# Linear attention's states: the order of the update and query matmuls, the engines of the first copies

## The chip, the cores and the metric

The kernel runs on one core of one Trainium2 chip. The metric is the device time of one execution in microseconds (us), as the median of some runs. Besides, one execution is profiled; its span is the time from its first to its last instruction.

## What is computed

A model of two blocks. The first block has a layer of gated linear attention with a dense feed-forward, then a layer of sliding-window attention with a mixture of eight experts; the second block is two layers of another attention. 256 tokens, width 1024. The change touches only the linear attention, in which the tokens are cut into four chunks of 64 and a state goes through the chunks, once forwards and once backwards (cut to what matters):

```python
def gla_chunked(q, k, v, log_a, inclusive):          # 4 heads, dk 128, dv 256, C = 64, n = 4 chunks
    ...
    chunk_update = jnp.einsum('bhnjk,bhnjv->bhnkv', k * jnp.exp(b_last - b), v)
    chunk_decay = jnp.exp(b_last[:, :, :, 0])
    def step(state, inp):
        decay, upd = inp
        return state * decay[..., None] + upd, state
    ...
    o_inter = jnp.einsum('bhnik,bhnkv->bhniv', q * jnp.exp(b), prev)
    return (o_intra + o_inter).reshape(B, H, S, dv)

o_f = gla_chunked(q, k, v, log_a_f, True)
o_b = flip(gla_chunked(flip(q), flip(k), flip(v), flip(log_a_b), False))
o = (o_f + o_b).transpose(0, 2, 1, 3)
o = o * lax.rsqrt(jnp.mean(o * o, axis=-1, keepdims=True) + NORM_EPS)
...
```

## The kernel before, in words

The program is written out by hand: each engine has its own list of instructions, in program order, and waits on semaphores that the others raise. A stage is a set of five functions (pe, act, dve, pool, sp). Nothing plans the order; the order in these functions is the order on the engine. Names: PE is the matrix engine, ACT the scalar engine, DVE the vector engine.

Weights come by DMA into slots, are split by ACT (L182) into a high part and by DVE (L192) into a low part, and every product with weights is three matmuls (`mm3`, L359, L360, L361). Most of the span is that.

In the linear attention (`make_gla`) the products within a chunk come first and leave their sums in four PSUM banks, `ob` = 1 to 4, two heads to a bank (L653). Then come the states. `S` holds the state of direction d (0 forwards, 1 backwards), 256 columns for each of four heads. There are three steps s. In step s direction 0 takes chunk c = s, direction 1 takes chunk c = 3 - s.

- PE `grow(s, d)` (L658): four matmuls, one a head, each over the 64 tokens of chunk c. They lie in partitions 0 to 63 where c is even and 64 to 127 where it is odd. The results go to PSUM banks 5 and 6 (d = 0) or 7 and 0 (d = 1), two heads to a bank. This is called an update block below (L668).
- DVE `grow(s, d)` (L822): in step 0 it copies the four results into `S` (L832), later it computes S x decay + result (L834). It raises `S_out(s, d)`.
- PE then multiplies the queries of the next chunk nx by `S` and adds the products to `ob` (L681). nx is s + 1 or 2 - s; the result has 64 columns of the array, and lies in PSUM partitions 0 to 63 or 64 to 127 by nx. This is called a query block below. It raises `crossed(s, d)`. All of it is in fp32 and each of these matmuls leaves two records in the trace.

PE's order is: update block (0,0), update block (0,1), and then for each s and d: query block (s,d), update block (s+1,d). Twelve blocks of four matmuls in all, and within each all four matmuls have the same chunk.

After the states, ACT squares the sums for the head norm, for tokens 128 to 255 first (j = 1, L439, waits for `crossed(2, 0)`) and then for tokens 0 to 127 (j = 0, waits for `crossed(2, 1)`). ACT and DVE make the inverse roots (L445, L449, L453), DVE scales (L846, `og`), PE transposes `og` (L418), ACT and DVE take the transposed parts into `xh` and `xl` (L424, L430), and PE goes on with the output projection (`gla out0`). ACT loads its table for the square root ahead of time (L763).

Two other places are spoken of. The scores of the sliding-window attention are written head after head, for each the three matmuls of `mm3` (L359, L360, L361) in turn; the first two of four heads lie in partitions 0 to 63, the other two in 64 to 127. And L708 is ACT's copy of a 128x256 result of PE out of PSUM.

Of the kernel before, what the change touches and what calls it, by code (L numbers as in the profile page):

```python
# [12 lines left out]
ACT = mybir.ActivationFunctionType  # L13
ALU = mybir.AluOpType
AX = mybir.AxisListType.X

D, T, FF, NE = 1024, 256, 2816, 8
# [108 lines left out]
def count_on(steps, names):  # L126

    return Steps(steps.sem, names, max(steps.n.values()))
# [71 lines left out]
def run(steps):  # L200
    for _ in steps:
        pass
# [8 lines left out]
def body(nc, ctx, I, out):  # L211
    count = [0]

    def sem(name):
        return ctx.enter_context(nc.semaphore(name))

    def steps(name, *names):
        return Steps(sem(name), names)
# [5 lines left out]
    psum = ctx.enter_context(nc.psum_tensor("psum", [128, 8, 512], F32))  # L224
# [320 lines left out]
    def make_gla(sc):  # L545
        qT = sb("qT", [128, 4, T], scope=sc)
        kT = sb("kT", [128, 4, T], scope=sc)
        v = sb("v", [128, 2, D], scope=sc)
# [7 lines left out]
        S = sb("S", [128, 2, D], scope=sc)  # L556
# [11 lines left out]

        ld_wg, s_wg0, s_sco0, s_one = sem("wg_landed"), sem("wg_zeroed"), sem("sco_zeroed"), sem("lr_one")
        DJ = [(d, j) for d in range(2) for j in range(2)]  # L570
        SD = [(s, d) for s in range(3) for d in range(2)]
        four = [(i,) for i in range(4)]
        q_out, k_out, lr_out = steps("gla_q", *four), steps("gla_k", *four), sem("gla_lr")
        z_acc, z_out = steps("gla_z_acc", *four), steps("gla_z", *four)
# [5 lines left out]
        prods = steps("gla_prods", *[(d, x) for d in range(2) for x in (0, 1, "k", "q", "kl", "qb")])  # L580
        intra = steps("gla_intra", *[(d, j, x) for d in range(2) for x in ("scores", "kl") for j in range(2)])
        sc_out, klN_out = steps("gla_sc", *DJ), steps("gla_klN", *DJ)
        o_acc, grown, S_out, crossed = sem("gla_o"), steps("gla_grown", *SD), steps("gla_S", *SD), steps("gla_crossed", *SD)

        OG = (4, 5, 6, 7, 0, 1, 2, 3)
        OB = (5, 6, 7, 3, 4, 2)
# [5 lines left out]

        def ch(ap):
            return ap.rearrange("p (g c) -> p g c", c=64)

        def sp(sp):
            for dst, src in ((wg[96:112, 0, :], I["gla_gate_w_fwd"][0]), (wg[112:128, 1, :], I["gla_gate_w_bwd"][0]),
# [13 lines left out]
        def pe(pe):  # L611
# [43 lines left out]
                                      start=h % 2 == 0, stop=False, skip_group_check=True)  # L655
            ins.then_inc(o_acc)

            def grow(s, d):  # L658
                c = s if d == 0 else 3 - s
                pp, j = (c % 2) * 64, c // 2  # L660
                bk = [5, 6] if d == 0 else [7, 0]
                pe.wait_ge(klN_out.at(d, 1), v_at)
                for h in range(4):
                    if s:
                        pe.wait_ge(S_out.at(s - 1, d))
                    else:
                        pe.wait_ge(klN_out.at(1, h // 2) if d == 0 else sc_out.at(1, h // 2))
                    ins = pe.e.matmul(psum[:, bk[h // 2], (h % 2) * 256:(h % 2) * 256 + 256],  # L668
                                      klN[pp:pp + 64, d, j, h * 128:(h + 1) * 128],
                                      v[pp:pp + 64, j, h * 256:(h + 1) * 256], start=True, stop=True)  # L670
                ins.then_inc(grown.end(s, d))

            grow(0, 0)
            grow(0, 1)
            for s in range(3):
                for d in range(2):
                    nx = s + 1 if d == 0 else 2 - s
                    op, oj = (nx % 2) * 64, nx // 2
                    pe.wait_ge(S_out.at(s, d), *qb_at[d])
                    for h in range(4):  # L680
                        ins = pe.e.matmul(psum[op:op + 64, ob[oj * 2 + h // 2], (h % 2) * 256:(h % 2) * 256 + 256],  # L681
                                          qb[:, d, h * T + nx * 64:h * T + nx * 64 + 64], S[:, d, h * 256:(h + 1) * 256],
                                          start=False, stop=True, skip_group_check=True)
                    ins.then_inc(crossed.end(s, d))
                    if s < 2:
                        grow(s + 1, d)
            free = {2: [og_out.at(3)], 3: [og_out.at(5)], 4: [og_out.at(7)], 5: [S_out.at(2, 0)], 6: [S_out.at(2, 0)],
                    7: [S_out.at(2, 1)]}
            turn(pe, "gla out", [(og[:, j, :], 128, j * 128) for j in range(2)], [[og_out.at(1)], [og_out.at(3)]], free, OB)
            y = x_is("gla out")  # L690
            run(moving_steps(pe, "gla out0", [0, 128], [0, 1], y, [[S_out.at(2, 1)], [og_out.at(1)]]))
            out1 = moving_steps(pe, "gla out1", [0, 128], [4, 5], y, [[y(4)], [y(6)]])
            next(out1)
            next(out1)
# [4 lines left out]
        def act(act):  # L699
# [22 lines left out]
            def column(i, dst, c, bk, func, out_):  # L722
                for j, mark in enumerate(done(f"gla vr{i}", 2)):
                    act.wait_ge(mark)
                    if func == ACT.Copy:
                        ins = act.e.activation(dst[:, j, c:c + 512], psum[:, bk[j], :], ACT.Copy, scale=1.0)
                    else:
                        ins = act.e.activation(dst[:, j, c:c + 512], psum[:, bk[j], :], func, bias=0.0, scale=1.0)
                    ins.then_inc(out_.end(c // 512, j))
# [25 lines left out]
            for d in range(2):  # L755
                for j in range(2):
                    act.wait_ge(intra.at(d, j, "kl"))
                    act.e.activation(klN[:, d, j, :], psum[:, 5 + j, :], ACT.Copy, scale=1.0).then_inc(klN_out.end(d, j))
                if d == 0:
                    W.hi_to(act, P["gla vr3"] + 1 + NS)  # L760
                    column(3, sr, 512, [3, 4], ACT.Silu, r_out)
            act.wait_ge(x(7), r_at)
            act.e.activation(st[:, 44:45], st[:, 0:1], ACT.Sqrt, bias=0.0, scale=1.0).then_inc(s_table.end("gla", -1))  # L763
            for j in (1, 0):
                srcs = [(psum[:, ob[j * 2 + h // 2], (h % 2) * 256:(h % 2) * 256 + 256], 128) for h in range(4)]
                squares(act, f"head{j}", 8 + 4 * j, srcs, junk[:, j * 1024:(j + 1) * 1024], (o_acc, 1), crossed.at(2, 1 - j), *qb_at[0],
                        *qb_at[1])
                root(act, f"head{j}", st[:, 8 + 4 * j:12 + 4 * j])
            high_by_gain(act, "gla out", T, G_HEAD, banks=OB)
# [7 lines left out]
        def dve(dve):  # L777
# [41 lines left out]
                if d == 0:  # L819
                    W.lo_to(dve, P["gla vr3"] + 1 + NS)  # L820

            def grow(s, d):  # L822
                c = s if d == 0 else 3 - s
                bk = [5, 6] if d == 0 else [7, 0]
                dve.wait_ge(grown.at(s, d))
                if s:
                    dve.wait_ge(crossed.at(s - 1, d), *qb_at[d], S_out.at(s - 1, d))
                for h in range(4):
                    o = S[:, d, h * 256:(h + 1) * 256]
                    u = psum[:, bk[h // 2], (h % 2) * 256:(h % 2) * 256 + 256]  # L830
                    if s == 0:
                        ins = dve.e.tensor_copy(o, u)  # L832
                    else:
                        ins = dve.e.scalar_tensor_tensor(o, o, dec[:, d, h * 4 + c:h * 4 + c + 1], u, ALU.mult, ALU.add)  # L834
                ins.then_inc(S_out.end(s, d))

            for s, d in SD:
                grow(s, d)
            for i in OG:
                j, h = i // 4, i % 4  # L840
                sl, n = slice(h * 256, (h + 1) * 256), f"head{j}"
# [7 lines left out]
            for half in range(2):  # L849
                W.lo_to(dve, P[f"gla out{half}"] + 1 + NS)  # L850
                out_add(dve, "gla", half, TOK, done(f"gla out{half}", 2))
                if half == 0:
# [1 line left out]
                    low_by_gain(dve, "dense", T, G_FFN[0], range(4), HB)  # L854

        ends = [W.passed(P["gla out1"] + 1), s_table.at("gla", 1), h_added.at("gla", 1, 1), (s_one, 1)]
        ended.extend([la_dve, la_act, q_out, k_out, z_acc, z_out, v_out, r_out, cum, b_out, exps, prods, intra, sc_out, klN_out,
                      grown, S_out])
        return Stage(pe, act, dve, pool, sp, ends)

# [2021 lines left out]
```

## Time and profile before

| | us |
|---|---|
| median of three runs | 1720.77 |
| lowest, highest | 1715.64, 1721.52 |
| the profiled execution | 1720.16 |
| its span | 1718.4 |
| PE busy in it | 1615.2 |
| DVE busy | 1221.8 |
| ACT busy | 1035.8 |

A row of the profile names a line of the kernel, an engine, an operation with the tiles that it writes and reads, the shapes, and a count. For PE two rows belong together: MATMUL (engine PE) and the weight load LDWEIGHTS (engine PEld), and the first number pair of their shape is the part of the array: 64*128 is 64 rows and all columns, 128*64 all rows and 64 columns. Times are in us from the start of the span; a matmul's own time includes its way through the array, so neighbours overlap in the records. Brackets give the idle time before a row and who ended it.

### The profile page before, as it was taken

Reading aid. Unit: us, or ns where it says so; the run is one execution under the profiler, and the core shown is the slowest. Engines: PE = TensorE matmul, PEld = TensorE weight load, DVE = VectorE, ACT = ScalarE, POOL = GpSimd, SP = SyncE. Lnnn points to the kernel's source line nnn. Section 1 sums busy time; section 2 is a strip of 40 time slices with the busy share of each in tenths; the row PEclk is TensorE's granted clock in tenths of the full one; section 3 lists DMA queues with packets and bytes.
Section 4 is the critical chain, followed back from the end, with each engine's and each line's share of the span. In section 5 each row is a group of like instructions: output and inputs, shape, how many; then the busy total and the mean of one; then the engine's idle time right before and its main releaser. Section 6 shows DMA issues by size and latency. Waiting matters only on the chain.

```text
span 1718.4 us, 21553 instructions
## 1 busy us (share of the span) xinstructions
PE 1615.2 (94%) x8649; PEld 1356.6 (79%) x8649; DVE 1221.8 (71%) x1299; ACT 1035.8 (60%) x1236; POOL 61.6 (4%) x71
## 2 busy tenths in 40 slices
PE   5999999988889999999999999999989998899987
PEld 5877788888778888888888878888868886788866
DVE  3655555468568888888888888888885576555665
ACT  4644544356567776776767767677775446454463
POOL 0000000014000000000000000000000200003000
PEclk9999999999989999999999999999998999899999
DMA  7422555552359999899999999999996532346410
GB/s 251 147 99 92 187 186 174 193 192 94 105 188 334 384 320 353 315 385 359 342 331 307 409 317 356 338 333 380 324 310 182 106 114 74 60 88 134 123 40 38
DMA packets 133080, 389.31 MB, mean 227 GB/s; under 512 B 8694, under 2 KB 14266, under 8 KB 132844
## 3 DMA queue, kind: packets, MB, share of 16 engines
q1 hardware_dynamic: 132692, 387.15, 66.1%
q8 instruction: 70, 1.15, 0.3%
q10 hardware_dynamic: 280, 0.70, 0.1%
q14 instruction: 38, 0.31, 0.1%
HBM read 386.78 MB, written 1.05 MB: 226 GB/s over the span
## 4 chain that ended last, share of the span: by engine, by line
PE 82%; DVE 7%; ACT 7%; issue 3%; DMA 0%; ACTq 0%; POOL 0%; DVEq 0%
PE psum L359 26%; PE psum L361 24%; PE psum L360 24%; DVE wlo L192 3%; ACT whi L182 3%; PE psum L1541 1%; PE psum L1593 1%; PE psum L2260 1%; PE psum L1135 0%; ACT hh L1653 0%; PE psum L2105 0%; PE psum L418 0%; PE psum L2246 0%; PE psum L2151 0%; PE psum L1622 0%
## 5 line engine op out<-in xcount | busy, mean ns | idle before, releaser
L192 DVE TENSOR_TENSOR wlo<-raw,whi 128x2048 fp32r<-128x2048 f32 (+1 forms) x286 | 629.5, 2213 | 217.6 <-ACT whi L182 216.8
L182 ACT ACTIVATE whi<-raw 128x2048 fp32r<-128x2048 f32 (+1 forms) x286 | 525.9, 1847 | 235.3 <-PE psum L361 235.3
L359 PE MATMUL psum<-whi,xh 128*128 128x512 f32 (+1 forms) x1280 | 497.9, 389 | 18.6 <-DVE xl L2606 9.9
L361 PE MATMUL psum<-whi,xl 128*128 128x512 f32 (+1 forms) x1280 | 486.4, 380 | 0.0
L360 PE MATMUL psum<-wlo,xh 128*128 128x512 f32 (+1 forms) x1280 | 484.9, 379 | 0.0
L359 PEld LDWEIGHTS psum<-whi,xh 128*128 128x128 f32 x1280 | 242.4, 189 | 75.3 <-issue 13.3
L361 PEld LDWEIGHTS psum<-whi,xl 128*128 128x128 f32 x1280 | 242.0, 189 | 49.3
L360 PEld LDWEIGHTS psum<-wlo,xh 128*128 128x128 f32 x1280 | 242.8, 190 | 45.6 <-issue 0.2
L192 DVE TENSOR_TENSOR wlo<-raw_more,whi 128x2048 fp32r<-128x2048 f32 (+1 forms) x94 | 204.0, 2177 | 38.9 <-ACT whi L182 38.2
L182 ACT ACTIVATE whi<-raw_more 128x2048 fp32r<-128x2048 f32 (+1 forms) x94 | 171.4, 1827 | 53.4 <-PE psum L361 53.4
L359 PE MATMUL psum<-xh,whi 128*128 128x256 f32 (+2 forms) x552 | 165.8, 300 | 16.8 <-DVE wlo L192 15.3
L359 PE MATMUL psum<-whi,hh 128*128 128x512 f32 x440 | 176.3, 401 | 1.1 <-DVE hl L977 1.1
L361 PE MATMUL psum<-whi,hl 128*128 128x512 f32 x440 | 173.2, 394 | 0.0
L360 PE MATMUL psum<-wlo,hh 128*128 128x512 f32 x440 | 172.4, 392 | 0.0
L361 PE MATMUL psum<-xh,wlo 128*128 128x256 f32 (+2 forms) x552 | 160.0, 290 | 0.0
L360 PE MATMUL psum<-xl,whi 128*128 128x256 f32 (+2 forms) x552 | 159.9, 290 | 0.0
L359 PEld LDWEIGHTS psum<-xh,whi 128*128 128x128 f32 (+1 forms) x552 | 105.6, 191 | 21.9 <-DVE wlo L192 15.5
L360 PEld LDWEIGHTS psum<-xl,whi 128*128 128x128 f32 (+1 forms) x552 | 105.6, 191 | 0.8
L361 PEld LDWEIGHTS psum<-xh,wlo 128*128 128x128 f32 (+1 forms) x552 | 105.1, 190 | 0.6
L361 PEld LDWEIGHTS psum<-whi,hl 128*128 128x128 f32 x440 | 82.6, 188 | 19.4
L359 PEld LDWEIGHTS psum<-whi,hh 128*128 128x128 f32 x440 | 82.7, 188 | 19.1 <-issue 1.3
L360 PEld LDWEIGHTS psum<-wlo,hh 128*128 128x128 f32 x440 | 82.9, 188 | 16.8
(362 smaller groups left out, 1503.9 us busy)
## 6 DMA issues: line engine op xcount, KB each, us to landing
raw<-in_moe_w_down_dram SPq DMA_DIRECT2D x58, 1024.0 KB, 7.7
raw<-in_moe_w_gate_dram SPq DMA_DIRECT2D x43, 1024.0 KB, 6.3
raw<-in_moe_w_up_dram SPq DMA_DIRECT2D x41, 1024.0 KB, 5.6
raw_more<-in_moe_w_down_dram SPq DMA_DIRECT2D x30, 1024.0 KB, 7.4
raw<-in_w_in_dram SPq DMA_DIRECT2D x28, 1024.0 KB, 8.0
raw_more<-in_moe_w_up_dram SPq DMA_DIRECT2D x23, 1024.0 KB, 5.6
raw_more<-in_moe_w_gate_dram SPq DMA_DIRECT2D x21, 1024.0 KB, 6.5
raw<-in_moe_w_up_dram SPq DMA_DIRECT2D x23, 768.0 KB, 4.8
```

The source lines that it names most:

```text
L182: act.e.activation(self.whi[:, i % self.ns, 0:kt * n], self.place[self.slots[i]][:, 0:kt * n], ACT.Copy, scale=1.0).then_inc(self.s_hi)
L192: dve.e.tensor_tensor(self.wlo[:, i % self.ns, 0:kt * n], self.place[self.slots[i]][:, 0:kt * n], self.whi[:, i % self.ns, 0:kt * n].bitca ...
L359: pe.e.matmul(o, lh, rh, start=start, stop=False)
L360: pe.e.matmul(o, lh, rl, start=False, stop=False)
L361: return pe.e.matmul(o, ll, rh, start=False, stop=stop)
L1541: ins = pe.e.matmul(psum[:, b, 0:N], half[:, j, k * 128:(k + 1) * 128], Pm[:, j, :], start=j == 0 and half is xnh, stop=j == 1 and half is ...
L1593: ins = pe.e.transpose(psum[:, b, j * 128:(j + 1) * 128], hid[:, c:c + 128], ident)
L2260: ins = pe.e.matmul(psum[0:m, 4, c], aT[:, u % 2, kt, 0:m], vvd[:, kt, c], start=kt == 0, stop=kt == NKT[nk] - 1)
```

## The change

PE's blocks no longer hold the four heads of one direction but two heads (hf = 0 or 1) of both directions, and within a block the two directions of a head are neighbours. The order of blocks is the same with hf in the place of d. In step 0 DVE copies the results of direction 0 and ACT, with a count of its own (`S_act`, on the semaphore of `z_acc`), those of direction 1; in the later steps DVE updates both directions of two heads. The waits follow: a block of hf waits for both directions of hf, and the squares of both j wait for the last query block, `crossed(2, 1)`. ACT's copies stand ahead of its table load. The number of matmuls, their shapes, operands and banks are the same.

```diff
+        SH = [(s, hf) for s in range(3) for hf in range(2)]
+        o_acc, grown, crossed = sem("gla_o"), steps("gla_grown", *SH), steps("gla_crossed", *SH)
+        S_out = steps("gla_S", *[(s, hf, d) for s, hf in SH for d in range(2) if s or not d])
+        S_act = count_on(z_acc, [(0,), (1,)])
...
+        def S_at(s, hf):
+
+            return S_out.at(s, hf, 0), (S_out.at(s, hf, 1) if s else S_act.at(hf))
+
+        def update_at(d, h):
+
+            return S[:, d, h * 256:(h + 1) * 256], psum[:, [[5, 6], [7, 0]][d][h // 2], (h % 2) * 256:(h % 2) * 256 + 256]
...
+            def grow(s, hf):
+                pe.wait_ge(klN_out.at(0, 1), klN_out.at(1, 1), v_at)
+                if s:
+                    pe.wait_ge(*S_at(s - 1, hf))
+                else:
+                    pe.wait_ge(klN_out.at(1, hf), sc_out.at(1, hf))
+                for h in (2 * hf, 2 * hf + 1):
+                    for d in range(2):
+                        c = s if d == 0 else 3 - s
+                        pp, j = (c % 2) * 64, c // 2
+                        ins = pe.e.matmul(update_at(d, h)[1], klN[pp:pp + 64, d, j, h * 128:(h + 1) * 128],
+                                          v[pp:pp + 64, j, h * 256:(h + 1) * 256], start=True, stop=True)
+                ins.then_inc(grown.end(s, hf))
+
+            def cross(s, hf):
+                pe.wait_ge(*S_at(s, hf), *qb_at[0], *qb_at[1])
+                for h in (2 * hf, 2 * hf + 1):
+                    for d in range(2):
+                        nx = s + 1 if d == 0 else 2 - s
+                        op, oj = (nx % 2) * 64, nx // 2
+                        ins = pe.e.matmul(psum[op:op + 64, ob[oj * 2 + hf], (h % 2) * 256:(h % 2) * 256 + 256],
+                                          qb[:, d, h * T + nx * 64:h * T + nx * 64 + 64], S[:, d, h * 256:(h + 1) * 256],
+                                          start=False, stop=True, skip_group_check=True)
+                ins.then_inc(crossed.end(s, hf))
 
             grow(0, 0)
             grow(0, 1)
...
+            for s, hf in SH:
+                cross(s, hf)
+                if s < 2:
+                    grow(s + 1, hf)
...
+            for hf in range(2):
+                act.wait_ge(grown.at(0, hf))
+                for h in (2 * hf, 2 * hf + 1):
+                    o, u = update_at(1, h)
+                    ins = act.e.activation(o, u, ACT.Copy, scale=1.0)
+                ins.then_inc(S_act.end(hf))
             act.wait_ge(x(7), r_at)
             act.e.activation(st[:, 44:45], st[:, 0:1], ACT.Sqrt, bias=0.0, scale=1.0).then_inc(s_table.end("gla", -1))
...
-                squares(act, f"head{j}", 8 + 4 * j, srcs, junk[:, j * 1024:(j + 1) * 1024], (o_acc, 1), crossed.at(2, 1 - j), *qb_at[0],
+                squares(act, f"head{j}", 8 + 4 * j, srcs, junk[:, j * 1024:(j + 1) * 1024], (o_acc, 1), crossed.at(2, 1), *qb_at[0],
...
+            def update(s, hf):
+                dve.wait_ge(grown.at(s, hf))
                 if s:
+                    dve.wait_ge(crossed.at(s - 1, hf), *qb_at[0], *qb_at[1], *S_at(s - 1, hf))
+                for d in range(2 if s else 1):
+                    c = s if d == 0 else 3 - s
+                    for h in (2 * hf, 2 * hf + 1):
+                        o, u = update_at(d, h)
+                        if s == 0:
+                            ins = dve.e.tensor_copy(o, u)
+                        else:
+                            ins = dve.e.scalar_tensor_tensor(o, o, dec[:, d, h * 4 + c:h * 4 + c + 1], u, ALU.mult, ALU.add)
+                    ins.then_inc(S_out.end(s, hf, d))
+
+            for s, hf in SH:
+                update(s, hf)
```

## Rows read from the trace of the kernel before

**Rows 1.** The page: span, busy time of each engine, chain that ended last

```profile
span 1718.4 us, 21553 instructions
PE 1615.2 (94%) x8649; PEld 1356.6 (79%) x8649; DVE 1221.8 (71%) x1299; ACT 1035.8 (60%) x1236; POOL 61.6 (4%) x71
...
PE 82%; DVE 7%; ACT 7%; issue 3%; DMA 0%; ACTq 0%; POOL 0%; DVEq 0%
```

**Rows 2.** Busy time by stretch (columns in the first row)

```profile
core 0: us, PE busy (x) PEld busy (x) DVE busy (x) ACT busy (x) POOL busy (x), PEclk, DMA share, GB/s
...
113.27:135.70 22.43, 21.89 (x97) 14.08 (x96) 9.49 (x25) 1.57 (x8) 0.00 (x0) 1.00 0.00 1
...
145.00:360.00 215.00, 210.43 (x987) 173.01 (x985) 107.30 (x83) 92.30 (x92) 0.00 (x0) 1.00 0.53 176
```

**Rows 3.** Timeline, PE and its weight loads: start, length, what, count [idle before]

```profile
113.28 2.96 PE L668 MATMUL psum<-v,klN 64*128 64x256 f32 x16
...
116.77 1.49 PEld L681 LDWEIGHTS psum<-S,qb 128*64 128x64 f32 x8 [0.94 <-DVE S L832]
...
118.65 1.99 PE L668 MATMUL psum<-v,klN 64*128 64x256 f32 x8
120.57 1.49 PEld L681 LDWEIGHTS psum<-S,qb 128*64 128x64 f32 x8 [0.33 <-issue]
120.57 1.94 PE L681 MATMUL psum<-S,qb 128*64 128x256 f32 x8
...
122.44 1.99 PE L668 MATMUL psum<-v,klN 64*128 64x256 f32 x8
...
131.94 3.76 PE L681 MATMUL psum<-S,qb 128*64 128x256 f32 x16
...
133.76 1.49 PEld L681 LDWEIGHTS psum<-S,qb 128*64 128x64 f32 x8 [0.33 <-DVE S L834]
```

**Rows 4.** Timeline, DVE in the same stretch (the last is one of three alike)

```profile
115.30 2.74 DVE L832 COPY S<-psum 128x256 f32<-128x256 f32 x8 [5.75 <-PE psum L668]
...
124.47 1.66 DVE L834 SCALAR_TENSOR_TENSOR S<-S,dec,psum 128x256 f32<-128x256 f32 x4 [2.14 <-PE psum L668]
```

**Rows 5.** Timeline from 113.9 us: it begins with the second record of L668

```profile
113.59 1.57 PE L668 MATMUL psum<-v,klN 64*128 64x256 f32 x9
```

**Rows 6.** Timeline, PE in the sliding-window attention's scores

```profile
401.02 0.28 PE L361 MATMUL psum<-kh,ql 64*128 64x256 f32 x1
401.03 0.39 PE L359 MATMUL psum<-kh,qh 64*128 64x256 f32 x2
401.25 0.28 PE L360 MATMUL psum<-kl,qh 64*128 64x256 f32 x2
401.37 0.29 PE L361 MATMUL psum<-kh,ql 64*128 64x256 f32 x2
```

**Rows 7.** Single instructions by line: ns min/median/max, first and last start

```profile
L668 PE MATMUL psum<-v,klN x48: 376/376/481, 113.3 to 131.6; 64*128 64x256 f32 x48
...
L681 PEld LDWEIGHTS psum<-S,qb x48: 132/137/137, 116.8 to 135.1; 128*64 128x64 f32 x48
...
L832 DVE COPY S<-psum x8: 414/414/424, 115.3 to 117.6; 128x256 f32<-128x256 f32 x8
...
L708 ACT ACTIVATE qT<-psum x4: 357/384/384, 31.8 to 35.7; 128x256 f32<-128x256 f32 x4
```

**Rows 8.** Timeline: ACT's table load, its first square, PE's and DVE's turn

```profile
110.36 1.28 ACT L763 ACT_TABLE_LOAD   x1
...
133.97 0.38 ACT L439 ACTIVATE bS<-psum 128x256 f32<-128x256 f32 x1 [22.12 <-issue]
...
139.37 3.37 PE L418 MATMUL psum<-cst,la 128*128 128x128 f32 x16 [3.67 <-DVE la L846]
...
140.61 3.40 DVE L430 SCALAR_TENSOR_TENSOR xl<-psum,pc,xh 128x256 fp32r<-128x256 f32 x8 [0.50 <-ACT xh L424]
```

**Rows 9.** Busy time by stretch, after PE's pause; PEclk is third from last

```profile
138.87:142.29 3.42, 2.92 (x14) 2.92 (x15) 2.92 (x8) 2.19 (x6) 0.00 (x0) 0.50 0.00 0
```

## What it should do to the time

> **What bounds the kernel now.** Start with the page. The span is 1718.4 us and PE is busy for 94% of it; the chain that ended last runs through PE for 82% [rows 1]. So a microsecond taken off PE, or off a wait that PE has, should be a microsecond off the whole, if nothing else is late behind it. The table of stretches then shows where the change lies. From 113.27 to 135.70 us PE is busy 21.89 of 22.43 us, while DVE works 9.49 us and ACT 1.57 us [rows 2]; then PE stands for 3.67 us and goes on [rows 8]. The change touches these 22.43 us, 1.3% of the span, and no DMA runs in them (share 0.00).
>
> Read the timeline of PE next [rows 3]. The stretch is twelve blocks of four matmuls; every matmul leaves two records, so a block is 8 records. Update blocks (L668) and query blocks (L681) alternate without idle time: 118.65, 120.57, 122.44, so an update block takes 1.92 us and a query block 1.87, together 3.79. DVE starts its four updates 0.04 us after the records of an update block end (122.44 + 1.99 = 124.43, start 124.47) and needs 1.66 us; before them it has waited 2.14 us for PE [rows 4]. So here PE's own pace is the limit. Making DVE faster would bring nothing in the steady part.
>
> How is a block's time made up? The last record of the update block starts at 118.65 + 1.99 - 0.376 = 120.26, so seven intervals take 1.61 us. In the first block the second record comes 0.31 us after the first (113.28, 113.59) [rows 5]; the other six intervals are then (1.61 - 0.32) / 6 = 0.215 each. The query block: 1.56 for seven, 0.27 and six of 0.215. From the last start of a block to the first of the next it is 0.31 (120.26 to 120.57), 0.09 more than an ordinary step, as the form goes from 64*128 to 128*64 and back [rows 3].
>
> **Part 1, the order of the matmuls.** Both kinds use half of the array: updates contract over 64 partitions, query products fill 64 columns. Before, all four matmuls of a block have the same half. The forward direction takes chunk s and the backward one 3 - s, so their halves are always opposite ones, and the change puts them side by side. Can two halves run at once? For rows the trace says yes, twice. The first two update blocks, of opposite halves, are adjacent today: 16 records in 2.96 us, last start 2.58 after the first [rows 3], where two blocks in turn would take 1.61 + 8 x 0.215 = 3.33. And in the sliding-window attention records of form 64*128 stand in twos: L360 x2 lasts 0.28 us in all, as one of them alone does, and the twos follow each other at 0.12 us [rows 6]. Each two is one record from each of two halves.
>
> So a paired update block has two halves with four records each: 0.32 + 2 x 0.215 = 0.75, plus the delay of the second half behind the first. That delay is 0.01 at the least (two records starting together) and 0.32 at the most (the second record's own delay); I take 0.20, between them, since the second weight load of a half comes about 0.1 us after the first and the other half's load is the third. It gives 0.95 instead of 1.61. For column halves no row shows two at once. The last two query blocks are adjacent and of opposite halves, but the second waits for DVE: its load has 0.33 us of idle time ahead of it, ended by S L834, and the 16 records take 3.76 us [rows 3]. The bounds are 1.56 us (no overlap) and 0.27 + 2 x 0.215 + 0.01 = 0.71; I take 0.90, the same construction as for rows, because the two are the same arrays split the other way. The number of changes of form stays at eleven, so 0.31 stays between blocks.
>
> In the attention stage the code writes L359, L360, L361 of one head and then of the next, yet two L360 run in one 0.28 us, and two L359 stand ahead of them after a single L361: a matmul of one half overtakes earlier ones of the other [rows 6]. And the eight loads of a query block, all for the same 128 rows, take 1.49 us within its 1.94 us: loads run beside matmuls there [rows 3].
>
> The page TensorE: Matmul & The Clock Gate of the Trainium skill (Part 3, The mechanism) says that matmuls start and end strictly in order, and that a weight load overlaps a running matmul only where the row group differs. This trace disagrees with both, by the two readings just given. By strict order a paired block would be about 0.14 longer (the last record at 1.09: 0.32, 0.01, 0.32, 0.215, 0.01, 0.215), some 1.4 us less gain over ten blocks; by the rule on loads the result would be rival (b).
>
> **Part 2, first copies on two engines.** Before, DVE makes 8 copies in 2.74 us: (2.74 - 0.414) / 7 = 0.33 each [rows 4, 7]. Afterwards a half has two copies on DVE (0.33 + 0.41 = 0.75) and two on ACT, bounded by ACT's 357 to 384 ns for this shape [rows 7], so ACT is never later than DVE by more than 0.02. ACT then stands idle for 22.12 us until 133.97 [rows 8]; the table load that is now queued behind these copies (1.28 us at 110.36) moves to about 116 and is hidden by eleven microseconds. If that cover were gone it would cost 1.5.
>
> **Part 3, the waits.** The products now wait for DVE and ACT of a whole half, and the update for both directions: four updates, 1.66 us as now. One loop of a half is 0.06 (DVE's end to PE: its fourth copy ends at 115.30 + 3 x 0.33 + 0.41 = 116.71, the loads start at 116.77 [rows 3, 4]) + 0.90 + 0.31 + 0.95 + 0.38 + 0.04 + 1.66 = 4.30 us; PE needs 2 x 2.47 = 4.94 for both halves. So PE stays the limit, with 0.6 us to spare, except at the end. One wait is added that costs: the squares of head row 1 (L439) wait for the very last query block and no longer for the last but one. At 133.97 they start 0.09 us after the first 8 of the 16 last records (131.94 + 1.94 = 133.88); in the new order nothing of PE is left beside them.
>
> **The sum**, in us from 113.28. Updates of step 0: 0 to 0.95 and on to 1.81. DVE's copies of the first half: 1.36 to 2.11. First query block at 2.17. From there each query and update block together 0.90 + 0.31 + 0.95 + 0.31 = 2.47: query blocks start at 2.17, 4.64, 7.11, 9.58, 12.05. The last update block starts at 10.79, its last record 11.74, DVE's last updates 12.15 to 13.81, the last query block 13.87, its last record 14.77, squares at 14.77 + 0.38 + 0.09 = 15.24. Today they start at 133.97 - 113.28 = 20.69. Gain 5.45 us. With the delay at 0.32 it is 4.5, with 0.01 about 6.3.
>
> **What is late next.** From the squares to the transposes everything hangs on ACT and DVE in a fixed chain (133.97 to 139.37, 5.40 us [rows 8]); it is not changed. PE's idle time before the transposes grows from 3.67 to about 5.5 us. PE stopped at 135.70 (131.94 + 3.76), and from 138.87 to 142.29 the granted clock is 0.50, its lower level of 1.2 GHz [rows 9]; the 16 transposes take 3.37 us in it. With a longer idle time the slow stretch can start before the transposes and end earlier or later. Ending earlier brings up to 1.0 (the banks then wait for DVE at 3.40 us for eight), ending one such stretch (3.42 us) later costs half of it, 1.7. I put it at +0.5, since a longer pause makes the fall surer than in an ordinary run of today. After that PE is busy 210.43 of 215.00 us between 145 and 360, with DMA at 0.53 of its time [rows 2], and for 94% of the whole [rows 1]: work goes at PE's pace, and the gain is carried along.
>
> The profiled execution took 1720.16 us, 1.8 more than its span and 0.6 less than the median of the three. 1720.16 - 5.45 + 0.5 = 1715.2; against the median 1715.8. I say 1715.5.
>
> **Rivals.** (a) Column halves do not overlap, only row halves do. Query blocks stay at 1.56: pairs of blocks 3.13, the last query block from 16.51 to 18.07, squares at 18.54, gain 2.1: 1718. For it: no row shows columns together. (b) Column halves get in each other's way, the slower side. Place: the six query blocks, where loads (137 ns [rows 7]) and matmuls of neighbouring halves go one after the other, 0.137 + 0.215 = 0.35 per record, 2.47 a block. Then the squares come at 9.14 + 6 x 2.47 = 24.0 (9.14 is all that is not query blocks: 2.17 + 4 x 1.57 + 0.22 + 0.47), 3.3 later than today: 1723.5. It decides from 9.14 + 6q = 20.69, q = 1.93, a step of 0.275 where it is 0.223 today. Against it: loads overlap matmuls within a block today. By the skill's rule for weight loads, named above, this case would hold. (c) The change doesn't do what it says: no pair overlaps, PE needs its 22.4 us as before, and the squares now wait for the last block, 1.8 later: 1722. Against it the two row readings. (d) The forecast's overlap holds, but the half clock reaches into the output projection: 1.7 more, 1717.
>
> **How the numbers follow.** Forecast 0.62, (a) 0.18, (b) 0.06, (c) 0.04, (d) 0.10. The runs lie from 1715.64 to 1721.52, 5.1 below their median and 0.8 above; that scatter is as large as the gain. Low end 1711 (the forecast with a run as low as the lowest), high end 1720 (case (a) with scatter); (b) and (c) are left out. 0.5%, about what a measurement of this kernel can tell from no change, is 8.6 us: below 1712.2 or above 1729.4. Every case lies inside; only scatter reaches below. Faster 0.10, same 0.88, slower 0.02.
>
> **What would show it.** L668 and L681 of both directions starting within 0.01 to 0.3 us of each other; 8 records of a query block in about 1.3 us instead of 1.94, of an update block in about 1.33 instead of 1.99; DVE's idle time before an update falling from 2.14 to about 0.8; squares at about 128.5; PE idle 5.5 us before L418. Query blocks still at 1.9 would be (a), at 2.8 (b); L668 still at 1.99 would be (c); L359 behind the transposes at 0.44 a step would be (d). I am wrong if the loop over DVE turns out longer than PE's, or if the matmuls of a half are issued slower than they run.

## The result, and the profile after

The changed kernel took 1707.31 us (median of 4 runs, 1705.49 to 1710.77) against 1720.67 before; the ratio is 0.9926, 95% interval 0.9911 to 0.9941. Two later comparisons gave 0.9944 (0.9931 to 0.9957) and 0.9936 (0.9923 to 0.9950). Over all 15 runs the mean is 1709.6, over all 112 runs of the kernel before 1719.8: 10.2 us less, give or take 1.1. The forecast was 1715.5, in a range of 1711 to 1720.

First the page of the changed kernel, beside [rows 1]:

```profile
span 1707.0 us, 21561 instructions
PE 1603.8 (94%) x8649; PEld 1347.0 (79%) x8649; DVE 1221.0 (72%) x1295; ACT 1037.9 (61%) x1240; POOL 61.7 (4%) x71
```

The profiled execution took 1708.78 us, 11.38 less than that of before. Four of DVE's instructions became ACT's. Then the timeline of the changed stage, beside [rows 3], [rows 4] and [rows 8]:

```profile
112.65 2.00 PE L678 MATMUL psum<-v,klN 64*128 64x256 f32 x16
...
113.83 0.66 ACT L778 ACTIVATE S<-psum 128x256 f32<-128x256 f32 x2 [4.11 <-PE psum L678]
113.83 1.62 DVE L849 COPY S<-psum 128x256 f32<-128x256 f32 x4 [4.91 <-PE psum L678]
...
114.64 1.08 PE L688 MATMUL psum<-S,qb 128*64 128x256 f32 x8
...
115.37 1.28 ACT L781 ACT_TABLE_LOAD   x1
...
115.66 1.14 PE L678 MATMUL psum<-v,klN 64*128 64x256 f32 x8
...
117.73 1.13 PE L678 MATMUL psum<-v,klN 64*128 64x256 f32 x8
118.80 0.63 PEld L688 LDWEIGHTS psum<-S,qb 128*64 128x64 f32 x8 [0.33 <-DVE S L851]
118.80 1.08 PE L688 MATMUL psum<-S,qb 128*64 128x256 f32 x8
118.92 1.66 DVE L851 SCALAR_TENSOR_TENSOR S<-S,dec,psum 128x256 f32<-128x256 f32 x4 [0.42 <-PE psum L678]
...
124.88 1.08 PE L688 MATMUL psum<-S,qb 128*64 128x256 f32 x8 [0.84 <-DVE S L851]
126.05 0.38 ACT L439 ACTIVATE bS<-psum 128x256 f32<-128x256 f32 x1 [9.18 <-issue]
...
131.45 3.36 PE L418 MATMUL psum<-cst,la 128*128 128x128 f32 x16 [5.49 <-DVE la L863]
```

An update block of 8 records lasts 1.13 us (1.99 before), a query block 1.08 (1.94 before), and a pair of blocks 117.73 - 115.66 = 2.07 us (3.79 before). So the halves of rows and the halves of columns both run at once. The eight weight loads of a query block take 0.63 us. DVE now has only 0.42 us between its updates. The squares start 126.05 - 112.65 = 13.40 us after the first update block; before it was 20.69. The part that was changed gave 7.29 us. The first 0.03 us of one block of each kind show the pairs, here all records that have begun by then:

```profile
117.73 0.49 PE L678 MATMUL psum<-v,klN 64*128 64x256 f32 x2
...
118.80 0.44 PE L688 MATMUL psum<-S,qb 128*64 128x256 f32 x2
```

Two records have begun within that time, and together they last 0.49 us, where the first of a block alone takes 0.48: they start 0.01 us apart. The second row shows the same for columns (0.44, and 0.43 alone).

The granted clock around PE's pause, beside [rows 9]:

```profile
125.97:127.50 1.53, 0.00 (x0) 0.00 (x0) 0.00 (x0) 1.46 (x8) 0.00 (x0) 1.00 0.00 0
127.50:134.30 6.80, 2.85 (x14) 2.85 (x15) 5.54 (x16) 4.11 (x17) 0.00 (x0) 0.50 0.00 0
134.30:136.00 1.70, 1.70 (x10) 1.48 (x9) 1.70 (x5) 1.70 (x5) 0.00 (x0) 0.98 0.00 0
```

The clock is at its lower level for 6.8 us instead of 3.4, for more than half of it (PE is busy for 2.85) while PE stands. The transposes take 3.36 us as before (3.37), and the clock is back at 134.30, before the output projection starts: rival (d) does not hold in this execution.

Now the remainder. From the first transpose to the end it was 1718.4 - 139.37 = 1579.0 us before and is 1707.0 - 131.45 = 1575.5: 3.5 us less, in code that the change doesn't touch. Another 0.6 us came ahead of the stage (the first update block starts at 112.65 instead of 113.28). 7.3 + 3.5 + 0.6 is the 11.4 between the two profiled spans. The experiments had to tell what the 3.5 us are.

### The profile page after: what moved, and what is told of

Its sections match the earlier page's. It is cut to its first block, busy times and chain, and to the rows that moved or that the text cites. A ratio compares the mean times of both kernels' runs of the same rounds, so it can differ in the third digit from the quotient of the medians.

```text
span 1707.0 us, 21561 instructions
## 1 busy us (share of the span) xinstructions
PE 1603.8 (94%) x8649; PEld 1347.0 (79%) x8649; DVE 1221.0 (72%) x1295; ACT 1037.9 (61%) x1240; POOL 61.7 (4%) x71
## 4 chain that ended last, share of the span: by engine, by line
PE 82%; DVE 7%; ACT 7%; issue 3%; ACTq 0%; DMA 0%; POOL 0%; DVEq 0%
PE psum L359 26%; PE psum L361 24%; PE psum L360 24%; DVE wlo L192 4%; ACT whi L182 3%; PE psum L1558 1%; PE psum L1610 1%; PE psum L2277 1%; PE psum L1152 0%; PE psum L1639 0%; ACT hh L1670 0%; PE psum L1640 0%; PE psum L2263 0%; PE psum L2122 0%; PE psum L418 0%
```

## The experiments

All differences below are of mean times to 1719.8, the mean of the 112 runs of before; the plus-minus is a 95% interval worked out from the scatter of both. They are in the order of the questions. same_cols, same_rows and dve_copies ran once each (1713.8, 1715.0 and 1708.9 us); they are read by their traces and not by their times.

**Do halves at once explain the stage?** In three kernels the two directions use the same half, so that nothing can run at once. Chunk parity is left out of the partitions, and this part of the computation is another one.

```diff
 same_rows, in grow (update blocks):
-                        pp, j = (c % 2) * 64, c // 2
+                        pp, j = 0, c // 2
 same_cols, in cross (query blocks):
-                        op, oj = (nx % 2) * 64, nx // 2
+                        op, oj = 0, nx // 2
 same_both: both edits
```

> The changed order, but the query products of both directions go to partitions 0 to 63 (this part of the computation is another one), so only the update blocks can run side by side. If column halves overlap in the changed kernel and are what this takes away: query blocks of 8 records back to 1.94 us, update blocks stay at 1.14, a pair of blocks 2.95 instead of 2.08 us, the squares about 4 us later after the first update block than the 13.40 of the changed kernel. If the four records of each half were limited by their issue, less.

Its timeline of PE and the first square:

```profile
113.40 2.00 PE L678 MATMUL psum<-v,klN 64*128 64x256 f32 x16
...
120.20 1.13 PE L678 MATMUL psum<-v,klN 64*128 64x256 f32 x8
...
121.26 1.94 PE L688 MATMUL psum<-S,qb 128*64 128x256 f32 x8
...
131.05 0.38 ACT L439 ACTIVATE bS<-psum 128x256 f32<-128x256 f32 x1 [13.44 <-issue]
```

Query blocks are back at 1.94 us, and the squares come 131.05 - 113.40 = 17.65 us after the first update block, 4.25 more than 13.40.

> The changed order, but the updates of both directions take partitions 0 to 63 (this part is another one), so only the query products can run side by side: update blocks back to 1.99 us, the first two together 3.7 instead of 2.00, query blocks stay at 1.08, a pair of blocks 2.94 us; the squares about 5.5 us later than 13.40. With same_cols this tells how the gain splits between the two kinds of halves.

```profile
114.00 3.72 PE L678 MATMUL psum<-v,klN 64*128 64x256 f32 x16
...
120.58 1.08 PE L688 MATMUL psum<-S,qb 128*64 128x256 f32 x8
...
121.60 1.99 PE L678 MATMUL psum<-v,klN 64*128 64x256 f32 x8
...
132.47 0.39 ACT L439 ACTIVATE bS<-psum 128x256 f32<-128x256 f32 x1 [12.54 <-issue]
```

Here 132.47 - 114.00 = 18.47, 5.07 more. Columns are worth 4.25 us and rows 5.07.

> The changed order, but both directions take partitions 0 to 63 for the updates and write their products to partitions 0 to 63, so that this part of the computation is another one and nothing can run side by side in the array. Same count and shapes of matmuls. If running side by side is the whole gain: blocks of 8 records at 1.99 and 1.94 us as before, squares about 22.4 us + 0.1 after the first update block, 1.8 later than in the kernel before, 0.7 more because the first two blocks no longer overlap: about 2.5 us slower than before, ratio 1.0015. If the order or the two engines for the first copies bring something of their own: less than 20.69 us.

```profile
113.45 3.72 PE L678 MATMUL psum<-v,klN 64*128 64x256 f32 x16
...
136.17 0.38 ACT L439 ACTIVATE bS<-psum 128x256 f32<-128x256 f32 x1 [16.79 <-issue]
```

22.72 us: 9.32 more than 13.40, just 4.25 + 5.07, and 2.0 more than before (20.69), since the squares wait for the last block and the first two blocks no longer overlap. So halves at once are the whole gain of the stage: without them the new order, with the copies on two engines, costs 2.0. But its time was not 2 us above before: -0.1 +- 1.2 on the mean of 12 runs, ratio 0.9998 (0.9987 to 1.0009). Here too something behind the stage gave back about 2.

**The first copies on two engines.** Here all first copies are DVE's again.

```diff
-                for d in range(2 if s else 1):
+                for d in range(2):
...
-            for hf in range(2):
-                act.wait_ge(grown.at(0, hf))
...
-                ins.then_inc(S_act.end(hf))
```

> The changed kernel with all eight first copies on DVE, as before. DVE's four copies of a half take 3 x 0.33 + 0.41 = 1.41 us instead of 0.75, so the first query block starts 0.66 us later and everything behind it too, if PE is the limit from then on: squares at 14.06 instead of 13.40. If DVE has room between its updates it is made up for and costs nothing; if DVE were the limit of the loop, 1.3 us.

```profile
112.83 1.60 PEld L677 LDWEIGHTS psum<-v,klN 64*128 64x128 f32 x16 [0.33 <-issue]
...
114.02 2.74 DVE L842 COPY S<-psum 128x256 f32<-128x256 f32 x8 [4.91 <-PE psum L677]
...
115.54 1.08 PE L687 MATMUL psum<-S,qb 128*64 128x256 f32 x8 [0.70 <-DVE S L842]
...
126.94 0.39 ACT L439 ACTIVATE bS<-psum 128x256 f32<-128x256 f32 x1 [15.52 <-issue]
```

The first query block waits 0.70 us, and 126.94 - 112.83 = 14.11: the two engines for the copies are worth 0.71 us, as expected.

**Is the rest a matter of where the later stages lie?** Extra matmuls of PE ahead of the first update block, in the changed kernel (5 and 9 of them) and in the one before (2, 5 and 9).

```diff
+            pe.wait_ge(klN_out.at(0, 1), klN_out.at(1, 0), v_at)
+            for _ in range(5):
+                pe.e.matmul(psum[:, 5, :], sco[:, 0, 0:128], v[:, 0, 0:512], start=True, stop=True)
             grow(0, 0)
```

> The changed kernel itself, timed again beside the one before. From the traces the part between the first update block and the squares became 7.3 us shorter (20.69 to 13.40), against the 11.4 us between the two profiled spans. Theory A (the order of blocks gives 7.3; the rest, some 4 us, is where the half-clock stretches of the second block happened to fall in the few runs seen): over more runs the ratio moves towards 7.3 us, 0.9958, if not all the way. Theory B (work elsewhere is really shorter, because everything behind the stage starts earlier against something fixed): the ratio stays at 0.9926, 12 to 13 us.

The median of its 6 runs is 1710.9, and their mean is 9.0 below the runs of before beside it: between the two theories.

> The changed kernel with five more 128x512 matmuls of fp32 ahead of the first update block (their result is overwritten), about 4.3 us of PE at full clock and no new idle time. Theory A: 4.3 us longer than the changed kernel, within the scatter of runs of 2 to 3 us. Theory B: a jump, since the later stages come to lie elsewhere: as much as 8 us longer, or hardly any.

> The same with nine such matmuls, about 7.7 us, which puts the output projection and all behind it where the kernel before had it. Theory A: 7.7 us longer than the changed kernel, so still some 5 us below the one before if the changed kernel stays 12 to 13 below it by chance, or level with it if that was chance of few runs. Theory B: the time of the kernel before, 12 to 13 us above the changed kernel.

Means -5.9 +- 0.9 and -3.4 +- 0.8, which is 4.3 and 6.9 above the changed kernel's -10.2, for 4.3 and 7.7 us put in. The changed kernel moves nearly as much as is put in, as theory A has it. But delay8 starts its transposes at 139.52, where before has 139.37, and is still 3.4 us below before.

> The kernel before, handed in like the others, so that its own runs and its own profile stand beside the runs of before. The means of the runs so far put the changed kernel 10.3 us below before, delay4 6.0, delay8 3.4 and same_both 0.1, where the part that was changed gives 7.3, 3.0, -0.5 and -2.1: all four are 2 to 4 us better than that. Theory A (the half-clock stretches behind the stage happen to fall worse for this kernel in many runs): equal to before within 1.5 us, and a profile whose part from the head of the output projection to the end lies near the 1579 us of the changed ones in some runs and up to 3 us above in others. Theory C (a run that is handed in is faster than the runs of before beside it, for a reason of the measurement): 2 to 3 us below before.

Mean -0.5 +- 1.6 (-0.6 against the other 100 runs): nothing like the 2 to 3 us of theory C shows, though the interval just reaches 2. Its profile shows how much the same code differs from run to run behind the stage:

```profile
span 1714.2 us, 21553 instructions
...
139.15 3.68 PE L418 MATMUL psum<-cst,la 128*128 128x128 f32 x16 [3.68 <-DVE la L846]
```

1714.2 - 139.15 = 1575.0 us from the transposes to the end; the other profile of the same kernel had 1579.0. So the 3.5 us lie within what two executions of one kernel differ by. The stretches of the second block in which the clock differs, first in the profile of before, then in this one (columns as in [rows 2]):

```profile
1384.00:1388.00 4.00, 3.07 (x13) 2.82 (x14) 3.93 (x7) 1.05 (x5) 0.00 (x0) 0.59 0.52 109
1500.00:1508.00 8.00, 6.67 (x20) 5.42 (x21) 3.04 (x11) 1.02 (x5) 0.00 (x0) 0.57 0.46 131
1603.00:1607.00 4.00, 4.00 (x22) 3.91 (x22) 2.66 (x3) 0.40 (x1) 0.00 (x0) 0.57 0.74 204
```

```profile
1384.00:1388.00 4.00, 3.65 (x29) 3.21 (x30) 3.93 (x9) 1.15 (x6) 0.99 (x2) 1.00 0.66 160
1500.00:1508.00 8.00, 7.80 (x30) 6.34 (x30) 2.48 (x10) 1.75 (x7) 0.00 (x0) 0.79 0.46 131
1603.00:1607.00 4.00, 4.00 (x35) 3.74 (x33) 2.08 (x7) 1.78 (x7) 0.00 (x0) 1.00 1.01 324
```

At 1384 and 1603 the clock fell in one execution and not in the other, while PE had work: at 1603 PE has 22 records in 4 us against 35. Where the 4 us lie is seen at ACT's table load between the two blocks (L1940, L1957 in the changed kernel), in before, before_again and the changed kernel:

```profile
1283.22 1.28 ACT L1940 ACT_TABLE_LOAD   x1
...
1282.78 1.28 ACT L1940 ACT_TABLE_LOAD   x1
...
1274.74 1.28 ACT L1957 ACT_TABLE_LOAD   x1
```

From the transposes to it they take 1143.9, 1143.6 and 1143.3 us, from it to the end 435.2, 431.4 and 432.3. Two more profiles of the changed kernel have 433.2 (after_again) and 432.2 (after_third) behind it. So most of the difference is in the second block, and before is the one that stands apart. The fall at 1603, 320 us behind the table load, stands in the profiles of before, before_delay2, before_delay4, before_delay8 and after_again, and in none of the other fifteen. Those five take 433.2 to 436.5 us from the table load to the end, the fifteen 430.2 to 433.1. The fall at 1384 doesn't sort them so: before_pause and delay8 have it too.

The runs of before fall in two groups, 25 of 112 below 1718 and most between 1719 and 1722. None of the 15 runs of the changed kernel is above 1712.2, where the upper group less 7.3 us would reach 1715.

> The kernel before with two more 128x512 matmuls of fp32 ahead of the first update block (result overwritten), 1.7 us of PE and nothing else. The changed kernels lie 2 to 4 us better than their changed part explains. Theory A (chance, or something in the changed order of blocks): 1.7 us above before, and no more. Theory B (how far the later stages lie from the start decides which half-clock stretches they meet, and before lies badly): not 1.7, but between level and 3 us below or as much above.

> The same with five matmuls, 4.3 us. Theory A: 4.3 above before. Theory B: well off 4.3, by 2 us or more; in the changed kernel five such matmuls cost 4.3 on the mean of the runs and nine cost 6.9 of 7.7, so the line there was nearly straight.

> The kernel before with nine more 128x512 matmuls of fp32 ahead of the first update block, 7.7 us of PE. Two such matmuls (1.7 us) cost 0.7 on the mean, five (4.3 us) cost 1.6. Theory A (only chance): 7.7 above before. Theory B (before lies badly against the half-clock stretches, and any shift helps): 4 to 6 above. In the changed kernel the same nine cost 6.9.

Means +0.7 +- 1.5 for 1.7 us, +1.5 +- 1.0 for 4.3 us, +6.9 +- 2.0 for 7.7 us. Five matmuls of 0.86 us each cost clearly less than they take; two and nine cost what they take, within their intervals. In the profile of before_delay4 it is the first block that is shorter: 1141.0 us from the transposes to the table load, where before has 1143.9. So the position behind the start can matter by some 3 us, but no rule comes out of it, and theory B doesn't explain delay8.

**Is it the pause of PE before the transposes?** It is 3.67 us in the kernel before and 5.49 in all changed ones. before_pause makes it longer in the kernel before, before_busy and busy_pause fill it with matmuls.

```diff
 before_pause, DVE, ahead of the first scaling:
+                    if j:
+                        for d, c in ((0, 0), (0, 512), (1, 0)):
+                            dve.e.tensor_tensor(kl[:, d, c:c + 512], kl[:, 1, 512:1024], kl[:, 1, 512:1024], ALU.mult)
 busy_pause (8 times) and before_busy (5 times), PE, behind the last query block:
+            for _ in range(8):
+                pe.e.matmul(psum[:, 5, 0:384], sco[:, 0, 0:128], v[:, 0, 0:384], start=True, stop=True)
```

> The kernel before with three products of 128x512 on DVE ahead of the first scaling (result not used), so that PE's pause before the transposes is some 2 us longer, 5.7 instead of 3.67 us as in the changed kernels, and nothing else. Theory P (the pause sets the clock's later falls): the time goes up by less than 2.0, to level with before or below. Theories A and B: 2.0 above before by A, anything by B.

Mean -1.7 +- 0.8, though the path got 1.7 us longer. Against the 24 runs of before beside it alone it is -1.5 +- 1.1, and the ratio is 0.9994 (0.9983 to 1.0004): that the 1.7 us were not paid is clear, that the kernel became faster is only just told. Theory P expected this much and no more. Span and transposes of its profile:

```profile
span 1715.9 us, 21556 instructions
...
141.37 1.97 PE L418 MATMUL psum<-cst,la 128*128 128x128 f32 x8 [5.33 <-DVE la L849]
```

The pause is 5.33 us, and from there to the end 1715.9 - 141.37 = 1574.5. The part behind the table load takes 431.8 of them, 3.4 less than in before. On the means, all but the pause is 3.3 us shorter than in before, and no run of twelve is above 1719.4. A longer pause also moves all that follows; before_delay2 moves it by the same 1.7 us without touching the pause, and lies 2.3 +- 1.6 us above before_pause. That is the size of what was unexplained in the changed kernels: 2.9 (10.2 - 7.3), and 2.1 in same_both (2.0 + 0.1).

> The changed kernel with eight 128x384 matmuls of fp32 in PE's pause between the last query block and the transposes (their result is overwritten), 5.1 us of the 5.5 us pause, so that the granted clock does not fall there. Transposes at full clock: 16 in about 2.6 instead of 3.36 us, the output projection about 1 us earlier after the squares. Theory A: about 1 us faster than the changed kernel. Theory C (the half-clock stretch of the pause sets where the later ones fall, and that is the 2 to 4 us nobody has explained): the tail behind the output projection becomes longer again, and the time goes up in spite of the faster transposes.

> The kernel before with five 128x384 matmuls of fp32 in PE's pause, so that no fall of the clock begins there. The transposes run at full clock, 1 us less where the clock has fallen today. Theory P: the mean moves by more than that, 3 us below before or more. Theories A and B: 0 to 1 us below.

Filling the pause keeps the clock up. In busy_pause the transposes show it:

```profile
132.48 2.35 PE L418 MATMUL psum<-cst,la 128*128 128x128 f32 x16
```

2.35 us instead of 3.36, and the output projection starts 1.0 us earlier against the first update block. The means are -11.5 +- 2.4 (changed kernel -10.2) and -2.3 +- 1.9. So theory C of busy_pause falls: without the half-clock stretch in the pause the tail does not become longer. before_busy is open; -2.3 fits a gain of 1 and one of 3. And since PE now works where it paused (5.43 us of matmuls in a pause of 5.5), it is not PE's idle time as such that makes the rest short: busy_pause has none there, and less the 7.3 of the stage and the 1.0 here its rest is 3.2 +- 2.4 us shorter than in before.

**A version meant to be better.** The squares of two heads start behind the last but one query block, all eight share one mean, root and reciprocal, and the scaling goes in the order in which the transposes need it.

```diff
+            for hf in range(2):
+                act.wait_ge(crossed.at(2, hf))
+                for j in (1, 0):
+                    for h in (2 * hf, 2 * hf + 1):
...
+            root(act, "head", st[:, 8:16])
...
-        OG = (4, 5, 6, 7, 0, 1, 2, 3)
+        OG = (4, 5, 0, 1, 6, 7, 2, 3)
```

> A version meant to beat both: the squares of two heads of both rows start after the last but one query block (as the first four did before the change), one mean, root and reciprocal for all eight, scaling in the order of the transposes' need, and six busy matmuls in the pause. ACT has 4 squares (1.4 us) instead of 8 behind the last query block, DVE one wait for ACT less (0.65 us). Transposes start at about 129.9 where the changed kernel has 131.45 (both with a first update block at 112.65): 1.5 us from the split and up to 1 us from the clock, 2 to 2.5 us below the changed kernel.

Mean -11.1 +- 1.8, median 1708.68. That is 0.9 us below the mean of the changed kernel, where 2 to 2.5 were expected, and 0.4 above that of busy_pause; neither difference can be told from none.

> The changed kernel with the squares split by heads, one mean, root and reciprocal for all eight, and the scaling in the order of the transposes' need, without busy matmuls. In split_busy the transposes began 5.12 us after the last query block where busy_pause had 6.58, 1.5 us less, and the output projection 0.5 us earlier against the start of the squares' block, since DVE's low parts then wait for all eight scalings. So 0.5 to 1.5 us below the changed kernel, on the mean about as split_busy (1708.7).

> The changed kernel once more. By its ten runs so far 10.2 us below before on the mean, 7.3 from the changed part and some 3 from what lies behind, as before_pause has shown for the kernel before (pause 1.7 us longer, all behind it 3.2 shorter). If that holds: 9.5 to 11 below. If the first runs were luck: 7 to 8.

> Split squares once more, in the same call. In its profile the transposes begin 1.45 us earlier behind the first update block than in the changed kernel, but the output projection's pace is set by DVE's low parts. 1 to 1.5 us below the changed kernel if nothing else moves, level with it if the shorter pause (4.0 instead of 5.5 us) gives the gain back as in the kernel before.

Timed side by side, the changed kernel had a median of 1709.8 (5 runs) and the split one 1708.87 (5 runs); over all runs the means are 1709.6 (15) and 1708.0 (11), 1.6 us apart, give or take 1.3. In the trace the transposes start 1.45 us earlier behind the first update block. Some 1.5 us, 0.1%, is what this version is worth: against before 0.9929 (0.9914 to 0.9945) and 0.9928 (0.9915 to 0.9942). It has the lowest mean of all kernels here, but is only just told from the changed one, and not from busy_pause (mean 1708.3).

## Why the prediction was wrong

**Right.** What bounds the stage (PE's order, not DVE), that halves of rows and of columns overlap, the eleven changes of form at 0.31 us, the new wait of the squares, the copies (0.71 measured, 0.66 from the same rows), the hidden table load, and that PE stays the limit until the last update. Rival (b), that neighbouring column halves get in each other's way, is refuted: same_cols shows 4.25 us lost when they can't overlap. The Trainium skill (TensorE: Matmul & The Clock Gate, Part 3, The mechanism) says that a weight load overlaps a running matmul only where the row group differs; the trace of the changed kernel disagrees: the loads of a query block, all for the same rows, take 0.63 us for eight, within 1.08 us of matmuls.

**The term that was mis-sized.** The delay of the second half behind the first was taken as 0.20 us, between 0.01 and 0.32. It is 0.01. A block's last record starts 1.13 - 0.376 = 0.75 us after its first where 0.95 was taken, and 1.08 - 0.379 = 0.70 where 0.90 was. A pair of blocks is 2.07 instead of 2.47, and the stage gives 7.3 instead of 5.45. The prediction named that low end and put the gain with it at about 6.3. This is a wrong sum: the delay stands in ten blocks one after the other, and with 0.01 in all of them the prediction's own chain puts the squares at 13.36 us, a gain of 7.3 (with 0.32 it is 4.25, not 4.5). Measured are 13.40 and 7.3. So with 0.01 in its place the sum of the stage is right to 0.04 us. The reason for 0.20, that loads would come one after the other at 0.1 us, was a guess from loads of one half. The attention rows [rows 6] had shown twos at 0.01 us, and they were the nearer row.

**The step that failed.** With the delay right and all else as forecast the time would have been about 1713.6, still inside the range; the step that took it out is another. "What is late next" put the longer pause at +0.5 us, with -1.0 to +1.7 as its ends. The transposes took 3.36 us as before. But all that follows was 2.9 us shorter on the mean of 15 runs, and 3.3 in before_pause, where only the pause was changed and the stage was not. The step priced the pause at its own place and took the scatter of the runs behind it as something that the change can't shift. That made the range end at 1711, where the measured median was 1707.3; the mean of all 15 runs, 1709.6, lies below it too. Of the 8.2 us between forecast and that median, 1.85 are the delay, 3.4 what lies behind the stage (+0.5 against -2.9), 2.3 the luck of the first four runs (their median against the mean of all 15), and the rest is the choice between mean, median and profiled run of before.

**What stays open.** Why the rest is shorter. The profiles show the place: the second block takes up to 4 us more in one execution of a kernel than in another, and the longest ones have a fall of the clock 320 us behind the table load that the others lack. They don't show why the change makes that fall rarer, if it does: two profiles of before and three of the changed kernel are too few. It is not the fall in the pause itself nor PE's idle time there (busy_pause has neither and keeps the gain), and not the position alone (delay8 lies where before lies and is 3.4 us faster).

## What to carry to other kernels

Where matmuls use half of the array, in rows or in columns, put neighbours of opposite halves next to each other in program order: the second starts 0.01 us behind the first, and here a pair of blocks took 2.07 us instead of 3.79. Price such a pair at the time of one, and then ask which engine is next; DVE had 0.42 us left between its updates.
In a kernel with many falls of the clock, what lies behind a change can become some 3 us shorter or longer though no line of it was touched. A difference of that size needs ten runs and more, and an experiment that moves only the pause.

## What the runs showed of the hardware

- Column halves of fp32 matmuls (128*64) run at once just as row halves (64*128) do: 8 records in 1.08 and 1.13 us instead of 1.94 and 1.99.
- A longer pause need not cost anything: 1.7 us more waiting of PE ahead of the transposes, 1.7 us less in all (+- 0.8; -1.5 +- 1.1 against the runs beside it).
- In 20 profiles, a half-clock stretch 320 us behind the table load goes with the long second blocks: 433.2 to 436.5 us with it, 430.2 to 433.1 without.
- 4.3 us of additional PE work ahead of the stage cost 1.5 us (+- 1.0) in the kernel before and 4.3 in the changed one.
- Filling a pause of PE with matmuls brought the 16 transposes behind it from 3.36 to 2.35 us.
